# The attention of the last mixer, with units of two heads in one branch instead of one head in two branches

## What is computed

```python
        p_s = masked_softmax(jnp.einsum('bqghd,bgqkd->bghqk', qr, k_sel), (kpos <= t[:, None])[:, :, None])
        o_s = jnp.einsum('bghqk,bgqkd->bqghd', p_s, v_sel)
...
        p_w = masked_softmax(jnp.einsum('bqghd,bkgd->bghqk', qr, kwin), m_w)
        o_w = jnp.einsum('bghqk,bkgd->bqghd', p_w, vwin)
        g = take(gates)
        o = g[..., 0:1] * o_c + g[..., 1:2] * o_s + g[..., 2:3] * o_w
```

## Time and profile before

| | us |
|---|---|
| median of 3 runs | 2651.84 (2641.0 to 2654.1) |
| the profiled execution | 2643.49 |
| its span, first to last instruction | 2641.7 |
| PE busy in the span | 2393.4 (91%) |
| DVE, ACT, POOL busy | 999.5, 724.8, 233.6 |
| the stage of this change, about 2002.5 to 2200.8 | 198.3 |
| PE busy in the stage | 152.30 |

### The profile page before, as it was taken

One profiled execution on the slowest core, in us unless ns is written; L12 is line 12 of the kernel. 1 busy time (PEld: TensorE's weight loads), 2 busy tenths in 40 slices (PEclk: granted clock), 3 DMA queues, 4 the chain that ended last, 5 costly groups with the idle time before them and its releaser, 6 DMA issues. The chain is left out here.

```text
span 2641.7 us, 32435 instructions
## 1 busy us (share of the span) xinstructions
PE 2393.4 (91%) x13850; PEld 1834.6 (69%) x13850; DVE 999.5 (38%) x1577; ACT 724.8 (27%) x1234; POOL 233.6 (9%) x255
## 2 busy tenths in 40 slices
PE   6978999988999989995789999999986777999997
PEld 3535556777888868884767888877864555788886
DVE  2013118534332326745133433423335443342333
ACT  2123200123222223313223322322113443342331
POOL 0003107300000000012000000000022430000000
PEclk8989999999999998986579999998987998999999
DMA  7120004311222112100012222212110003222210
GB/s 292 36 83 33 32 32 160 128 64 64 80 112 96 72 73 96 64 32 3 3 68 92 96 96 96 96 67 96 66 32 1 1 1 128 79 102 99 102 66 32
DMA packets 17119, 196.35 MB, mean 74 GB/s; under 512 B 2000, under 2 KB 3152, under 8 KB 5072
## 3 DMA queue, kind: packets, MB, share of 16 engines
q1 hardware_dynamic: 15824, 189.67, 19.3%
q10 hardware_dynamic: 1152, 4.61, 0.4%
HBM read 190.08 MB, written 2.10 MB: 73 GB/s over the span
## 5 line engine op out<-in xcount | busy, mean ns | idle before, releaser
L1585 DVE TENSOR_TENSOR wsp_mlp<-ring,wsp_mlp 128x1024 fp32r<-128x1024 f32 x128 | 156.8, 1225 | 438.6 <-ACT wsp_mlp L1547 438.6
L1547 ACT CAST wsp_mlp<-ring 128x1024 fp32r<-128x1024 f32 x128 | 134.3, 1049 | 349.8 <-PE psum L1532 345.4
L1529 PE MATMUL psum<-hs_mlp,wsp_mlp 128*128 128x512 f32 x512 | 201.9, 394 | 8.1 <-DVE hs_mlp L1418 8.1
L1529 PE MATMUL psum<-acts_mlp,wsp_mlp 128*128 128x512 f32 x512 | 202.4, 395 | 0.0
L1531 PE MATMUL psum<-hs_mlp,wsp_mlp 128*128 128x512 f32 x512 | 201.4, 393 | 0.0
L1532 PE MATMUL psum<-hs_mlp,wsp_mlp 128*128 128x512 f32 x512 | 201.1, 393 | 0.0
L1532 PE MATMUL psum<-acts_mlp,wsp_mlp 128*128 128x512 f32 x512 | 199.4, 389 | 0.0
L1531 PE MATMUL psum<-acts_mlp,wsp_mlp 128*128 128x512 f32 x512 | 199.3, 389 | 0.0
L1585 DVE TENSOR_TENSOR wsp_ffn<-ring,wsp_ffn 128x1024 fp32r<-128x1024 f32 x66 | 80.9, 1225 | 236.5 <-ACT wsp_ffn L1547 236.5
L424 PE MATMUL psum<-hsev,wspev 128*128 128x512 f32 x672 | 158.2, 398 | 3.9 <-DVE wspev L404 3.9
L424 PEld LDWEIGHTS psum<-hsev,wspev 128*128 128x128 f32 x672 | 129.6, 193 | 32.1 <-DVE wspev L404 4.7
(11 more groups left out here) (423 smaller groups left out, 4159.7 us busy)
## 6 DMA issues: line engine op xcount, KB each, us to landing
ring<-weights SPq DMA_DIRECT2D x85, 2048.0 KB, 7.9
ring<-weights SPq DMA_DIRECT2D x3, 1024.0 KB, 4.9
cst<-consts ACTq DMA_DIRECT2D x1, 2209.0 KB, 14.5
xT<-xin SPq DMA_DIRECT2D x2, 1024.0 KB, 6.8
ring<-weights SPq DMA_DIRECT2D x1, 1280.0 KB, 5.9
mixT<-ctxin ACTq DMA_DIRECT2D x1, 1024.0 KB, 15.1
ring<-weights SPq DMA_DIRECT2D x2, 512.0 KB, 3.5
arena<-arena_low SPq DMA_DIRECT2D x8, 128.0 KB, 2.3
```

The costliest lines, as they stand in the source:

```text
L1529: pe.matmul(tile_bank(g, j), w_hi, src[:, 0, k0 + i, :], start=(first and i == 0), stop=False)
L1547: act.copy(wsp[:, q % 2, 0, :], raw_view(q)).then_inc(s["w_hi"], 1)
L1585: dve.tensor_tensor(wsp[:, q % 2, 1, :], raw_view(q), wsp[:, q % 2, 0, :].bitcast(F32), ALU.subtract).then_inc(s["w_lo"], 1)
```

## The change

A unit `w` is now one step and one branch with both heads. There are twice as many, 64, in the order branch 0, branch 1 of each query block.

- The score banks are 2 br + par: branch 0 uses banks 0 and 1, branch 1 banks 2 and 3. `scores(w)` holds two matmuls and waits for exps(w-2).
- `lows` release ACT once for each head, not once for two; each exp waits for its own.
- `turn(w)` writes one bank for each head and counts `turn_done` after each; ACT copies the bank of head 0, DVE that of head 1. A turn waits for both copies of the unit before.
- `values(w)` holds the matmuls of one branch; the compressed branch goes with branch 1.
- DVE's `out` now also waits for the values of four units before.
- The orders become: PE scores(w+2), values(w-1), turn(w); DVE inverse(w+1), lows(w+2), out(w); ACT store (when w is 1 mod 8, from 9 on), exps(w+2), out(w).

```diff
-                def scores(v):
-                    t, j, i = steps[v]
-                    if v >= 1:
-                        pe.wait_ge(exp_done, 2 * v)
+                def scores(w):
+                    t, j, i, br = part_of(w)
+                    if w >= 2:
+                        pe.wait_ge(exp_done, w - 1)
...
+                def turn(w):
+                    i = part_of(w)[2]
+                    pe.wait_ge(prob_done, w + 1)
+                    if w >= 1:
+                        pe.wait_ge(turn_a, w)
+                        pe.wait_ge(turn_v, w)
...
                 scores(0)
-                for v in range(NV):
-                    if v + 1 < NV:
-                        scores(v + 1)
-                    if v >= 1:
-                        values(v - 1)
-                    turn(v, 0)
-                    turn(v, 1)
-                values(NV - 1)
+                scores(1)
+                for w in range(NW):
+                    if w + 2 < NW:
+                        scores(w + 2)
+                    if w >= 1:
+                        values(w - 1)
+                    turn(w)
+                values(NW - 1)
...
+                for w in range(NW):
+                    if w + 1 < NW:
+                        inverse(w + 1)
+                    if w + 2 < NW:
+                        lows(w + 2)
+                    out(w)
...
+                    for par in range(2):
+                        act.wait_ge(low_done, 2 * w + par + 1)
+                        last = act.activation(pp[:, w % 4, par, 0:n], bank(2 * br + par, n), ACT.Exp,
...
+                for w in range(NW):
+                    if w % 8 == 1 and w >= 8:
+                        store(w // 8 - 1)
+                    if w + 2 < NW:
+                        exps(w + 2)
+                    out(w)
```

More of the change, by code:

```diff
@@ L2628, in program @@
         steps = [(t, j, i) for t, j in pairs2 for i in range(TT)]
-        NV = len(steps)
+        NW = 2 * len(steps)
         score_done, low_done, exp_done, inv_done, prob_done = (
@@ L2632, in program, with part_of, turn_bank @@
         turn_done, turn_a, turn_v, pv_done, pv_out = (sem(n) for n in ("turn2", "turn_a2", "turn_v2", "pv2", "pv_out2"))
-        def turn_bank(u, br):
-            return 4 + (2 * u + br) % 3
+        def part_of(w):
+            return steps[w // 2] + (w % 2,)
+        def turn_bank(w, par):
+            return 4 + (2 * w + par) % 3
         with nc.Block() as block:
@@ L2639, in _ @@
             def _(pe):
-                def scores(v):
-                    t, j, i = steps[v]
-                    if v >= 1:
-                        pe.wait_ge(exp_done, 2 * v)
-                    for br in range(2):
-                        for par in range(2):
[L2646 to L2683, removed]
+                def scores(w):
[3 more added lines that the diff above has]
+                    for par in range(2):
+                        rows = slice(64 * par, 64 * par + 64)
+                        last = pe.matmul(bank(2 * br + par, (i + 1) * P), qr[rows, 4 * t + j, i * P:(i + 1) * P],
+                                         kr[rows, 2 * br + t, 0:(i + 1) * P], start=True, stop=True)
+                    last.then_inc(score_done, 1)
@@ new lines, in turn @@
+                def turn(w):
[4 more added lines that the diff above has]
+                        pe.wait_ge(turn_v, w)
+                    for par in range(2):
+                        for k in range(i + 1):
+                            last = pe.transpose(bank(turn_bank(w, par))[:, k * P:(k + 1) * P],
+                                                pp[:, w % 4, par, k * P:(k + 1) * P], ident)
+                        last.then_inc(turn_done, 1)
@@ new lines, in values @@
+                def values(w):
+                    t, j, i, br = part_of(w)
+                    pe.wait_ge(turn_a, w + 1)
+                    pe.wait_ge(turn_v, w + 1)
+                    if br == 0 and i == 0 and w >= 8:
+                        pe.wait_ge(pv_out, w // 8)
+                    blk = slice(32 * j, 32 * j + 31)
+                    for k in range(i + 1):
+                        for par in range(2):
+                            g = 2 * t + par
+                            out = psum[64 * par:64 * par + 64, 7 * 512 + i * P:7 * 512 + (i + 1) * P]
+                            last = pe.matmul(out, vtok[:, k, br * 256 + g * ND:br * 256 + (g + 1) * ND],
+                                             pT[w % 4][:, par, k, :], start=(br == 0 and k == 0), stop=False)
+                    if br == 1:
+                        for par in range(2):
+                            g = 2 * t + par
+                            out = psum[64 * par:64 * par + 64, 7 * 512 + i * P:7 * 512 + (i + 1) * P]
+                            last = pe.matmul(out, vcb[blk, g * ND:(g + 1) * ND], pcT[blk, g, i * P:(i + 1) * P],
+                                             start=False, stop=True)
@@ L2696, in _ @@
+                values(NW - 1)
             @block.vector
             def _(dve):
[L2698 to L2717, removed]
+                def lows(w):
+                    i, br = part_of(w)[2:]
+                    dve.wait_ge(score_done, w + 1)
+                    n = (i + 1) * P
+                    for par in range(2):
+                        s = bank(2 * br + par, n)
+                        dve.tensor_tensor_reduce(out=s, in0=s, in1=later[:, T - n:T], scale=1.0,
+                                                 scalar=-NEG, op0=ALU.add, op1=ALU.min,
+                                                 accum_out=st2[:, w, par:par + 1]).then_inc(low_done, 1)
@@ new lines, in inverse, with out @@
+                def inverse(w):
+                    dve.wait_ge(exp_done, w + 1)
+                    dve.reciprocal(st2[:, w, 4:6], st2[:, w, 2:4]).then_inc(inv_done, 1)
+                def out(w):
+                    i = part_of(w)[2]
+                    dve.wait_ge(turn_done, 2 * w + 2)
+                    if w >= 4:
+                        dve.wait_ge(pv_done, w - 3)
+                    dve.tensor_copy(pT[w % 4][:, 1, 0:i + 1, :],
+                                    bank(turn_bank(w, 1), (i + 1) * P).rearrange("p (k n) -> p k n", n=P))\
@@ L2722, in _ @@
                 dve.wait_ge(later_set, 2)
-                lows(0, 0)
-                lows(0, 1)
+                lows(0)
+                lows(1)
                 inverse(0)
[L2726 to L2736, removed]
+                for w in range(NW):
[4 more added lines that the diff above has]
+                    out(w)
@@ L2738, in _ @@
             @block.scalar
             def _(act):
[L2740 to L2748, removed]
-                    last.then_inc(exp_done, 1)
@@ L2751, in out, with exps @@
[L2751 to L2757, removed]
+                def exps(w):
+                    i, br = part_of(w)[2:]
+                    if w >= 4:
+                        act.wait_ge(turn_done, 2 * (w - 4) + 2)
+                    n = (i + 1) * P
+                    for par in range(2):
+                        act.wait_ge(low_done, 2 * w + par + 1)
+                        last = act.activation(pp[:, w % 4, par, 0:n], bank(2 * br + par, n), ACT.Exp,
+                                              bias=st2[:, w, par:par + 1], scale=-1.0,
+                                              accum_out=st2[:, w, 2 + par:3 + par])
+                    last.then_inc(exp_done, 1)
@@ L2759, in store, with out @@
+                def out(w):
+                    i = part_of(w)[2]
+                    act.wait_ge(turn_done, 2 * w + 1)
+                    if w >= 4:
+                        act.wait_ge(pv_done, w - 3)
+                    act.copy(pT[w % 4][:, 0, 0:i + 1, :],
+                             bank(turn_bank(w, 0), (i + 1) * P).rearrange("p (k n) -> p k n", n=P)).then_inc(turn_a, 1)
                 def store(pair):
                     t, j = pairs2[pair]
-                    act.wait_ge(pv_done, 4 * pair + 4)
+                    act.wait_ge(pv_done, 8 * pair + 8)
@@ L2778, in _ @@
             def _(pool):
[L2779 to L2786, removed]
+                for w in range(NW):
+                    t, j, i, br = part_of(w)
+                    n = (i + 1) * P
+                    pool.wait_ge(inv_done, w + 1)
+                    for par in range(2):
+                        h = 4 * (2 * t + par) + j
+                        last = pool.tensor_scalar(pp[:, w % 4, par, 0:n], pp[:, w % 4, par, 0:n],
+                                                  st2[:, w, 4 + par:5 + par], gates[:, i, 3 * h + 1 + br:3 * h + 2 + br],
+                                                  ALU.mult, ALU.mult)
                     last.then_inc(prob_done, 1)
```

## The result

| | before | after |
|---|---|---|
| median of 7 runs, us | 2645.46 (2638.13 to 2654.1) | 2621.06 (2615.07 to 2630.78) |
| the profiled execution, us | 2643.49 | 2617.71 |
| its span, us | 2641.7 | 2615.9 |
| the stage, first score matmul to last store, us | 198.2 | 173.3 |
| pitch of 512-wide scores, us | 22.76, or 24.0 to 24.4 | 20.67 |

The pitch is the time from the first 512-wide score group of one pair of heads, scores(3.0), to that of the next pair. Stage, pitch and clock level are read from the one profiled execution of each kernel.

What follows compares the result with a forecast made beforehand. It took no engine as full and a loop of waits, scores, lows and exps through shared banks, as the pace; 1.5 + 7 x 1.49 + 0.2 + 7.5 = 19.6 us gained gave 2630 us, range 2608 to 2650.

Steps and rivals of the forecast that it cites:

- PE's own work: TensorE's groups per pair of heads at full clock: 18.48 us after the change, 16.94 before.
- The fixed 0.2 us of each group: Cost on PE at each change from one kind of group to the next, charged for six groups per block.
- the first rival: Nearly all PE waits in the stage vanish: gain 28 to 42 us, about 2616 us; chance 0.12.
- The stands in the new round: PE's waits in one pair after the change, mostly for copies before values: 2.79 us, making 21.27 us a pair.
- The walk: Hand-traced after order of PE, DVE and ACT through one pair of heads, giving 21.27 us against 22.76.
- Start and end: Gains at the stage's start, up to the first 512-wide scores (1.5 us), and at its end (0.2 us).
- The clock: All five drops of TensorE to its lower clock level in 512-wide score groups vanish: 7.5 us gained.
- The second rival: The clock drops in the stage stay: gain 12 us, about 2638 us; chance 0.16.
- the slower one: Rival: 21 or more stretches at 1.2 GHz, each costing 1.6 us, make it over 0.5% slower, about 2666; chance 0.06.
- Sum: Total gain forecast from start, seven pairs, end and clock: 1.5 + 7 x 1.49 + 0.2 + 7.5 = 19.6 us.
- What bounds the kernel now: In the stage no engine is full; scores, lows, exps through shared banks set the 22.76 us round of a pair.
- The third rival: The ring turn, DVE copy, inverse, lows, exps, ACT copy, values binds everywhere: gain 4 us, about 2646; chance 0.08.

Runs made afterwards that it cites:

- the filled kernel: Kernel before, with idle transposes between the two turns of the 256-wide (8), 384-wide (8) and 512-wide (5) blocks; stage 190.8 us, ratio 0.9982.
- the run without the alternation: Changed kernel, with scores(w) waiting for the exps of w-1 instead of w-2; stage 199.6 us, program 2649.74 us in its one run.
- the run with paired lows: Changed kernel, with both exps of a unit waiting for both lows; pitch 22.38 us, program 2637.68 us in its one run.

## Why the prediction was right, point by point

**PE's own work** (18.48 us a pair after the split): the kernel with values two units behind runs the same groups with no stand at all, in 18.53. The fixed 0.2 us of each group was a real cost, and the first rival, that it was the tail of a wait, is out.

**The stands in the new round** (2.79 us): six of the eight places were right, with sizes too long by 0.04 to 0.18 us. Forecast and measured: 0.83 and 0.79, 0.59 and 0.51, 0.38 and 0.30, 0.43 and 0.25 (the store), 0.23 and 0.12, 0.11 and 0.07; the stands forecast before values(2.0) (0.14) and values(1.1) (0.08) did not occur. Measured are 2.04 us together, 0.75 less. The turns took 5.57 us a pair against the 5.40 charged, so the pair is 20.67 instead of 21.27 us, and 7 x 0.60 = 4.2 us of the surplus. The walk gave 0.15 to 0.2 us from a copy's end to PE; behind ACT's copy above it was 0.04.

**Start and end** (1.5 and 0.2): measured 1.9 (13.69 against 15.60 us from the first scores to scores(3.0)) and 0.9 (14.96 against 15.87 from the last 512-wide scores to the last store, without the drop at 2183.44, where those scores took 3.48 instead of 1.99 us).

**The clock** (7.5 us): no drop is left, and the filled kernel prices them at 7.4. The reason, a denser PE, fits the filled kernels, with two corrections: the thin stretch before the 512-wide scores was not the only one that lets the clock fall, and 2.6 us of work where the old pair had 1.7 was no proof that it holds, since it fell once behind 2.50 of 3.40 us in the run without the alternation. That all five drops went may be partly luck: one profile of the changed kernel can't tell. The second rival (the drops stay) and the slower one (more of them, at 1.6 us each) did not occur: PE ran at the upper level throughout once the first block was done. The oscillation that the Trainium skill (TensorE: Matmul & The Clock Gate, A second HAM failure mode) describes, cited for more of them, did not come in this kernel, though it too cycles through banks with small stands: the granted clock is 1.00 from 2017.70 to 2177.30.

**Sum**: 1.9 + 7 x 2.09 + 0.9 + 7.5 = 24.9, against 19.6. Every term but the clock came out larger than forecast, so no two errors cancelled.

**What bounds the kernel now** was half wrong. The text made the chain of scores, lows and exps through shared banks the pace of the whole round. Moving values between the turns, with that chain untouched, took 1.83 of 22.76 us a pair, all of it in the two rounds that start with the 128- and 256-wide scores. So there PE's own row of scores, values and turns with stands between was the pace; the chain can have been it only in the two wide rounds, which the move left as they were. The forecast did not suffer, since the new round was walked with both kinds of links. But a sum that had only subtracted a chain would have credited the banks with what the order gave. The third rival, the ring over DVE and ACT, came closer than its chance of 0.08 says: the run with paired lows shows that five of the eight units had next to no slack left against it.

**Left open**: whether the 0.2 us is the price of a change of tiling mode (half or full array) or of any change of group; and why the program outside the stage differs by up to some us between kernels that don't touch it.

## What to carry to other kernels

When engines run fixed lists, write down one round of the new order with its links before pricing it, and look for PE's stand behind the group just issued: work from another unit in that place hides the copy out, and one unit more of distance took another 2 us a pair. Splitting units to alternate banks cost a fixed 0.2 us per group here, and the halves without the alternation lost all of the gain; halves in the old order were not tried. Count what stands cost in clock beyond their length: here 7.4 us of 24.9 came from stands that no longer made the clock fall, and even useless transposes in those stands earned them in the stage. Before splitting units, try the order by itself: here one block of code moved gave over half of what the whole change gave in the stage.

## What the runs showed of the hardware

- The clock drops followed a thin stretch, not a line of the program: with the stand of the 256-wide block filled, four drops came behind the 384-wide block instead (1.74 us busy in 3.4, then a granted clock of 0.51); with both filled there was none. Thin stretches of the same kind held the clock in other pairs, so each is only a risk. The stretch need not be very thin: in the run without the alternation the clock fell once behind 2.50 us of work in 3.40, a stretch with no stand over 0.70.
- In the kernel with three stands filled, eight idle transposes took 1.04 us in a stand of 1.3 us and moved nothing behind them: the 512-wide scores still came 3.0 us after the first of these turns, at 2063.70 as before.
- With values two units behind, PE ran groups of three kinds (scores, values, turns) back to back, busy 18.53 of 18.53 us with a granted clock of 1.00; its weight loads were busy 11.63 us of that, beside the matmuls.
